# Splitting half a weight chunk ahead of the pair eviction in the FFN of a two-layer float32 decoder trunk

## What is computed

```python
x = _layer_norm(DN_ALPHA * x + mix_out, ln1_g[l], ln1_b[l])
gate_up = jnp.einsum('bld,df->blf', x, ffn_w_gate_up[l])
f_gate, f_up = jnp.split(gate_up, 2, axis=-1)
ffn_out = jnp.einsum('blf,fd->bld', jax.nn.silu(f_gate) * f_up, ffn_w_down[l])
x = _layer_norm(DN_ALPHA * x + ffn_out, ln2_g[l], ln2_b[l])
```

## Time and profile before

| what | value |
|---|---|
| median of 3 runs | 3080.51 us (3078.68 to 3080.82) |
| the profiled execution | 3077.45 us, of which its span is 3075.7 us |
| TensorE busy | 2984.2 us, 97% of the span |
| VectorE busy | 2060.0 us, 67% |
| ScalarE busy | 1453.3 us, 47% |
| mean granted TensorE clock | 0.990 of full speed |
| transfers | 562.16 MB, 183 GB/s mean |

### The profile page before, as it was taken

One profiled execution on the slowest core, in us unless ns is written; L12 is line 12 of the kernel. 1 busy time (PEld: TensorE's weight loads), 2 busy tenths in 40 slices (PEclk: granted clock), 3 DMA queues, 4 the chain that ended last, 5 costly groups with the idle time before them and its releaser, 6 DMA issues.

```text
span 3075.7 us, 46726 instructions
## 1 busy us (share of the span) xinstructions
PE 2984.2 (97%) x16182; PEld 2544.8 (83%) x16182; DVE 2060.0 (67%) x3164; ACT 1453.3 (47%) x1967; POOL 146.4 (5%) x200
## 2 busy tenths in 40 slices
PE   6999999999999999999999999999999999999996
PEld 5888888888788888888878888888878888888885
DVE  5999766665766555555699986666667555566556
ACT  4556554554444444444455655455444444444442
POOL 5000011110000000000000000000000000000002
PEclk9999999999999999999999999999999999999998
DMA  8656567676555555555555556767745555555553
GB/s 268 168 147 169 157 179 202 178 205 205 203 186 191 185 191 191 179 188 179 187 145 154 152 154 178 202 176 197 229 164 190 180 190 190 189 175 191 183 190 123
DMA packets 672969, 562.16 MB, mean 183 GB/s; under 512 B 20760, under 2 KB 637568, under 8 KB 671872
## 3 DMA queue, kind: packets, MB, share of 16 engines
q1 hardware_dynamic: 668688, 548.48, 59.1%
q10 hardware_dynamic: 4208, 12.74, 1.1%
HBM read 552.78 MB, written 8.39 MB: 182 GB/s over the span
## 4 chain that ended last, share of the span: by engine, by line
PE 84%; DVE 7%; ACT 3%; issue 2%; POOL 1%; DMA 1%; ACTq 1%; DVEq 0%; POOLq 0%
PE banks L1452 23%; PE banks L1467 18%; PE banks L1455 11%; PE banks L1469 9%; PE banks L1477 6%; PE banks L1479 5%; PE banks L1478 5%; DVE lo L981 3%; PE banks L1745 2%; ACT hi L641 2%; DVE hh L1417 1%; DVE hh L1413 1%; PE banks L1747 1%; ACT pt L939 1%; DVE st L1132 1%
## 5 line engine op out<-in xcount | busy, mean ns | idle before, releaser
L981 DVE TENSOR_TENSOR lo<-raw,hi 128x1024 fp32r<-128x1024 f32 x1016 | 1214.5, 1238 | 274.1 <-ACT hi L641 242.1
L641 ACT ACTIVATE hi<-raw 128x1024 fp32r<-128x1024 f32 x884 | 890.1, 1051 | 353.7 <-PE banks L1479 236.1
L1467 PE MATMUL banks<-xs,hi 128*128 128x512 f32 x2816 | 893.1, 399 | 10.9 <-DVE lo L981 10.5
L1452 PE MATMUL banks<-xs,hi 128*128 128x512 f32 x2544 | 807.2, 399 | 3.5 <-DVE lo L981 2.2
L1469 PEld LDWEIGHTS banks<-xs,lo 128*128 128x128 f32 x2816 | 531.4, 189 | 125.7
L1455 PEld LDWEIGHTS banks<-xs,lo 128*128 128x128 f32 x2544 | 478.6, 188 | 113.1
L1469 PE MATMUL banks<-xs,lo 128*128 128x256 f32 x2816 | 555.6, 279 | 0.0
L1455 PE MATMUL banks<-xs,lo 128*128 128x256 f32 x2544 | 500.7, 278 | 0.0
L1467 PEld LDWEIGHTS banks<-xs,hi 128*128 128x128 f32 x2816 | 432.5, 190 | 17.6 <-DVE lo L981 16.0
L1452 PEld LDWEIGHTS banks<-xs,hi 128*128 128x128 f32 x2544 | 388.6, 189 | 15.0 <-issue 11.1
L1477 PE MATMUL banks<-hi,hT 128*128 128x512 f32 x704 | 276.6, 393 | 8.3 <-DVE lo L981 8.3
(11 more groups left out here) (213 smaller groups left out, 2710.4 us busy)
## 6 DMA issues: line engine op xcount, KB each, us to landing
raw<-in_ffn_w_gate_up SPq DMA_DIRECT2D x176, 1024.0 KB, 5.1
raw<-in_w_in SPq DMA_DIRECT2D x160, 1024.0 KB, 7.6
raw<-in_ffn_w_down SPq DMA_DIRECT2D x88, 1024.0 KB, 5.3
raw<-in_w_o SPq DMA_DIRECT2D x32, 1024.0 KB, 5.5
raw<-in_mem_w_kv SPq DMA_DIRECT2D x16, 1024.0 KB, 5.6
raw<-in_sb_w_out SPq DMA_DIRECT2D x32, 512.0 KB, 4.1
raw<-in_ssm_w_out SPq DMA_DIRECT2D x32, 256.0 KB, 4.5
raw<-in_mem_w_out SPq DMA_DIRECT2D x32, 256.0 KB, 4.8
```

The source lines that it names most:

```text
L641: act.activation(hi[:, hl_slot(ph, c, h), :], raw[:, slot, h * HALF:(h + 1) * HALF], ACT.Copy).then_inc(hi_ready, 1)
L981: dve.tensor_tensor(lo[:, s, :], raw[:, slot, h * HALF:(h + 1) * HALF], hi[:, s, :].bitcast(F32), ALU.subtract).then_inc(lo_ready, 1)
L1452: pe.matmul(dst[:, :], hi[:, s, k * P:(k + 1) * P], x_t[:, k0 + k, :], start=first and k == 0, stop=False)
L1467: pe.matmul(bank[base + j], hi[:, s, at[j]], xs[:, k, :], start=k == 0, stop=False)
```

## The change

ACT and DVE split the first half of chunk c + 2 ahead of the eviction of the pair that ends with chunk c, in place of behind it. The second half of chunk c + 2 stays behind it. It is done for c = 1, 3, 5 and 7 in every turn of both layers, 88 times in all. Nothing is added or removed: both engines issue the same instructions in another order, and SP's and TensorE's programs are unchanged. Line numbers behind the edit move by 3 (ACT's part, and all of DVE's part ahead of its own edit) and by 10 behind DVE's.

```diff
@@ ACT, ffn_turn
                             if not last_l:
                                 for h in range(2):
                                     hi_half("U", l + 1, 0, 0, h)
+                        elif c in (2, 4, 6, 8):
+                            hi_half("FF", l, i, c + 1, 1)
                         elif not (first and c == 0):
                             split_next("FF", l, i, c)
                         if c < 8 and c % 2:
                             q, a = c // 2, c // 4
+                            hi_half("FF", l, i, c + 2, 0)
                             act.wait_ge(half_done, done("FF", l, i, c))
@@ DVE, ffn_turn
                     n = i + 11 * l
+
+                    def lo_ahead(c, h):
+                        lo_half(PHASES["FF"][1][c], hl_slot("FF", c, h), h, chunk_no("FF", l, i, c) * 2 + h)
+
                     for c in range(12):
...
+                        elif c in (2, 4, 6, 8):
+                            lo_ahead(c + 1, 1)
                         elif not (first and c == 0) and not (last and c == 10):
                             split_next("FF", l, i, c)
...
                         if c < 8 and c % 2:
                             q, a = c // 2, c // 4
                             src = banks[:, PAIR_BANK[q]:PAIR_BANK[q] + 2, T:2 * T]
+                            lo_ahead(c + 2, 0)
                             dve.wait_ge(ffn_step, n * 4 + (2 * a + 1 + q % 2))
                             dve.wait_ge(first_out, tile_no("FF", l, i, q) + 1)
```

## The result

The changed kernel takes 3053.18 us (median of 4 runs, 3049.85 to 3055.38) against 3079.73 us before on the same chip: a ratio of 0.9914 with a 95% interval from 0.9902 to 0.9927, which is 26.5 us less (22 to 30). The forecast was 3057.1. Run again later beside other kernels it took 3054.09 against 3079.24, again 0.9914 [0.9898, 0.9931]. The profiled execution took 3053.24 us, with a span of 3051.5 us, 24.2 less than before.

The account below looks back on a forecast made before the run. TensorE, with 84% of the chain, was taken as the bound, so only its waits for DVE's low halves could be won. Loop turns 21.1, turn 10 1.9 and turn 0 0.4 sum to 23.4 us: 3080.51 becomes 3057.1, range 3052 to 3063.

Parts of the forecast that it names:

- The waits of the loop turns: Turns 1 to 9, behind pair 1 and at chunk 9: both waits for low halves go, 1.17 us a turn, 21.1 us.
- The rival that something else holds TensorE there: Loop turns: something the semaphore's name hides holds TensorE, the 1.17 us come back each turn; 3080 us, chance 5%.
- The slack of what was pushed: Loop turns: the moved half leaves slack of 1.7 us at `pt`, 1.1 at `uu`, 1.0 at chunk 9.
- the rival on the slow side: Every turn, at pair 3: late data block the eviction and `hT`; 3107 us at 3.5 us of delay; chance 5%.
- Turn 10: Written-out turn of each layer: shorter waits behind pair 1 and at chunk 9 go, 0.95 us each, 1.9 us for two.
- Turn 0: First turn of each layer: earlier load helps, blocked eviction harms; 0.2 us won each, 0.4 us for two.
- each of its four times: Turn 0, TensorE: chunk 7 at 838.26, its second half at 841.74, chunk 8 at 845.28, chunk 9 at about 850.9.
- the blocked eviction: Turn 0: pair 2's eviction waits behind high half (7, 0) for chunk 7's data, starting at 836.85 instead of 830.50.
- The earlier load: Turn 0: the second residual ends 1.14 us earlier, and so do chunk 7's issue and arrival.
- a loss of 1.0 us: Turn 0, chunk 7 to chunk 9: TensorE goes from 838.26 to about 850.9, with late low halves and late `hT`.
- chunk 7's two extra stops: Turn 0, TensorE stops at chunk 7's second half (841.17 until 841.74) and at chunk 8 (844.64 until 845.28).
- the signs named for being wrong: Loop turn staying near 67.5 us, `pt` over 0.3 us behind the pair's end, or FFN clock below 1.00.

Follow-up runs that it names:

- experiments with up pairs: Changed kernel with the first half moved ahead of the eviction only behind chunks 3 and 7: 3049.91 us, ratio 0.9908 to the kernel before.
- gate pairs alone: Changed kernel with the first half moved ahead of the eviction only behind chunks 1 and 5: 3079.85 us, ratio 1.0002 to the kernel before.
- the experiment with both halves: Changed kernel, but behind chunks 3 and 7 both halves of chunk c + 2 are split ahead of the eviction: 3070.52 us, ratio 0.9968 to the kernel before.
- Turns 1 to 10 alone: The change made only in turns 1 to 10, turn 0 keeping the order of before: 3057.33 us, ratio 0.9929 to the kernel before.

## Why the prediction was right

**The waits of the loop turns** were most of it, as argued. The turn went from 67.51 to 66.37 us, the forecast 66.4. The sizes hold because they were taken from the starts of matmuls with the slow restart counted (0.11 us each), not from the idle figure of the waits view: that gives 0.20 + 0.40 = 0.60 a turn, half of what was won. Both waits follow up pairs; the experiments with up pairs and gate pairs alone show it. The rival that something else holds TensorE there is out.

**The slack of what was pushed** was read rightly: 1.7 us ahead of `pt` were reckoned and 1.80 of idle time are left; `uu` has 1.18 for 1.1; and ahead of chunk 9 it is about 0.85 for 1.0, by the experiment with both halves. This is the mechanism of the rival on the slow side. Even with 1.5 us of delay in every turn it took only 17 us back, and the kernel stayed faster than before.

**Turn 10** was 0.95 us each by rows 7; in the changed kernel its waits are gone. Turns 1 to 10 alone gave 22 us for the 23.0 expected of them and the loop together.

**Turn 0** was worked out move by move, and in the first layer of the profiled execution each of its four times came out within 0.15 us, the blocked eviction at 838.60 - 1.70 = 836.90 among them (836.85 was reckoned). What the Trainium skill says in "TensorE: Matmul & The Clock Gate" (Part 1), that ScalarE is a strict FIFO, agrees with this row: the eviction, whose pair had ended 7.0 us before (831.62), ran right behind the half that waited for its data.

**The term that was too small** is turn 0's: 0.4 us for both, measured at about 2 to 3. Between the changed kernel and the one with turns 1 to 10 alone there are 3.2 us (four runs each, whose ranges just meet). The mean distance to chunk 9 is 64.0 us in four turns with the old order (before, and turns 1 to 10 alone) against 63.0 in four with the new one (the changed kernel twice), with one short stretch of half clock in the norm on either side: 2.0 us for both layers. The earlier load gave what was reckoned, a mean of 1.16 for 1.14. From chunk 7 to chunk 9 the prediction has a loss of 1.0 us, from 11.64 to 12.64, and measured are 12.80 with the old order and 12.97 with the new, a loss of 0.17. The step of the prediction that was mis-sized is this loss: I worked turn 0 out on the first layer alone and took its clock of 1.00 for both. The trace of before already had the other case in layer 1. Its windows view, in the stretch behind the wait at chunk 7:

```profile
2346.00:2349.50 3.50, 3.50 (x14) 2.98 (x13) 3.47 (x4) 2.00 (x2) 0.00 (x0) 0.55 1.02 408
```

There chunk 7 took 7.24 us instead of 5.70. In the changed kernel, chunk 7's two extra stops bring it to 7.09 with a full clock, and a halved clock hides them at 7.25. So where the clock falls, the harm reckoned for the blocked eviction does not add up with the clock's, and the 1.14 us of earlier loading are won. The one exception is the 8.44 us of the second execution, where the clock was low for longer. The rest of the 3.1 us between the gain forecast, 23.4, and the 26.5 measured is within the interval of the ratio.

One of the signs named for being wrong did come: the clock in the FFN fell below 1.00, to 0.50 in the second layer's turn 0. It was badly chosen, since the kernel before shows the same fall there. It does not speak against the mechanism of the loop turns, where the clock stayed at 1.00, but it marks the place where the account of turn 0 was incomplete.

## What to carry to other kernels

In a queue that works in order, put work whose input is ready early ahead of the work that waits for the end of a stage, and keep behind it what becomes ready only at that end: the first filled a gap of 4.6 us at no cost in the loop turns, and the second cost 0.74 us a turn. Before doing so, look for the one turn in which the moved work's data come late, since there it blocks all that stands behind it. Such a turn is also where to look for more: issuing one load ahead of a transfer that waits for another engine won 9 to 10.5 us, more than a third of the change's gain again, without touching the loop.

## What the runs showed of the hardware that was not expected

Behind the waits of 2.6 to 4.6 us at chunk 7 the granted clock fell to the 1.2 GHz level in 11 of the 16 cases of the eight traces that have such a wait, and stayed full in the other five (waits of 3.37, 2.66, 2.66, 2.73 and 2.77 us). A wait of 3.36 us was followed by a fall and one of 3.37 was not, and the same place in the same execution differed between the layers, so the length of the wait alone does not decide it in this range. In ten of the 11 cases it fell 0.1 to 1.4 us after TensorE had resumed and stayed low for about 3.4 us, and chunk 7 took 7.23 to 7.26 us in place of 5.70. In the eleventh, the second layer of the changed kernel's second execution, it fell 0.8 us before the restart and stayed low for 6.8 us, and chunk 7 took 8.44. In the six cases without a wait the clock stayed at 1.00.
